# Expert 0's rows from a one-hot product in SBUF, and expert 0 run through before expert 1 starts

## What is computed

```python
h = rms_norm(x, norm_ffn_g)                      # 512 x 1024
g_idx = argmax(softmax(h @ w_rg + b_rg))         # one of 4 groups
top_p, top_i = top_k(softmax(expert logits of that group), 2)   # 2 of its 8 experts
for e in range(32):                              # rows given to expert e
    y = (silu(xb @ w1[e]) * (xb @ w3[e])) @ w2[e]    # w1, w3: 1024x512, w2: 512x1024
    out[rows of e] += weight * y
```

## Time and profile before

| | us |
|---|---|
| runs | 1755.36, 1760.81, 1761.26 |
| median | 1760.81 |
| the profiled execution, its own time | 1759.36 |
| its span, first to last instruction | 1757.8 |
| TensorE busy | 1610.4 (92%) |
| DMA, mean over the span | 185 GB/s |
| mean granted TensorE clock, share of full | 0.955 |

### The profile page before, as it was taken

The page is one execution under the profiler, slowest core; times in us unless marked ns, Lnnn a source line. Parts: engine busy times, 40 slices in busy tenths (PEclk is TensorE's granted clock), DMA queues, the critical chain, the costliest instruction groups (busy, mean ns, idle before and its releaser), DMA issues.

```text
span 1757.8 us, 15347 instructions
## 1 busy us (share of the span) xinstructions
PE 1610.4 (92%) x5808; PEld 792.1 (45%) x5808; DVE 723.0 (41%) x1529; ACT 478.5 (27%) x980; POOL 363.3 (21%) x348
## 2 busy tenths in 40 slices
PE   7998999999999699988888787899989999999998
PEld 3434456644554333333333333444455554445553
DVE  2856434264242312110110110549775143987612
ACT  2022242101121101100000001566366134735621
POOL 3800000001000111111211110148243012842500
PEclk9998999999999799998898888999999999999999
DMA  9511032457255599999999999602102130020101
GB/s 332 191 49 48 0 120 96 144 191 252 72 214 222 195 401 406 406 406 410 407 404 398 412 414 359 227 1 72 72 1 91 49 113 1 23 98 25 48 0 48
DMA packets 72401, 325.98 MB, mean 185 GB/s; under 512 B 10458, under 2 KB 13682, under 8 KB 59904
## 3 DMA queue, kind: packets, MB, share of 16 engines
q1 hardware_dynamic: 64976, 310.23, 45.3%
q0 software_dynamic: 6144, 10.52, 1.8%
q10 hardware_dynamic: 1200, 4.17, 0.6%
HBM read 320.60 MB, written 12.68 MB: 190 GB/s over the span
## 4 chain that ended last, share of the span: by engine, by line
PE 71%; DMA 21%; DVE 5%; ACT 2%; issue 1%; POOL 0%; SPq 0%; POOLq 0%; DVEq 0%; ACTq 0%
PE bank L190 67%; DMA arena<-in_w 16%; DMA arena<-x_rows,arena 3%; PE bank L2200 1%; DMA arena<-in_w_in 1%; DVE arena L2660 1%; DMA x_rows<-arena 1%; ACT arena L2375 1%; DVE arena L2647 0%; PE bank L680 0%; DVE arena L2662 0%; PE bank L929 0%; PE bank L2147 0%; DMA arena<-y_rows 0%; DMA y_rows<-arena 0%
## 5 line engine op out<-in xcount | busy, mean ns | idle before, releaser
L190 PE MATMUL bank<-arena 128*128 128x512 f32 (+10 forms) x4944 | 1507.8, 547 | 87.5 <-DMA arena<-in_w 51.1
L190 PEld LDWEIGHTS bank<-arena 128*128 128x128 f32 (+5 forms) x4944 | 689.0, 177 | 839.6 <-issue 780.3
L2822 POOL TENSOR_TENSOR arena<-arena 128x512 f32<-128x512 f32 x180 | 198.9, 1105 | 204.4 <-ACT arena L2428 186.7
L1834 DVE SCALAR_TENSOR_TENSOR arena<-arena,bank 64x512 f32<-64x512 f32 x32 | 24.0, 750 | 314.0 <-ACT arena L1247 314.0
L1891 POOL TENSOR_TENSOR arena<-arena 128x1 f32<-128x1 f32 (+2 forms) x44 | 34.2, 777 | 568.1 <-DVE arena L1282 341.3
L2428 ACT ACTIVATE arena<-arena 128x512 f32<-128x512 f32 x180 | 127.0, 725 | 21.1 <-POOL arena L2822 21.1
L1013 ACT COPY arena<-bank 128x512 f32<-128x512 f32 (+3 forms) x115 | 61.2, 539 | 234.1 <-PE bank L190 130.7
L1247 ACT ACTIVATE arena<-bank,arena 64x512 f32<-64x512 f32 x32 | 21.9, 684 | 362.2 <-PE bank L190 362.2
L1912 POOL DMA_INDIRECT y_rows<-arena x32 | 32.4, 1014 | 406.6 <-ACT arena L1258 245.7
L1294 DVE SCALAR_TENSOR_TENSOR arena<-arena 128x512 f32<-128x512 f32 x84 | 78.4, 933 | 2.7
L1827 DVE TENSOR_TENSOR arena<-bank,arena 128x512 f32<-128x512 f32 x32 | 22.1, 692 | 107.5 <-PE bank L929 107.5
(11 more groups left out here) (268 smaller groups left out, 898.1 us busy)
## 6 DMA issues: line engine op xcount, KB each, us to landing
arena<-in_w SPq DMA_DIRECT2D x96, 2048.0 KB, 39.8
arena<-in_w_in SPq DMA_DIRECT2D x15, 2048.0 KB, 9.4
arena<-in_w_ada SPq DMA_DIRECT2D x12, 2048.0 KB, 9.2
arena<-in_w_out SPq DMA_DIRECT2D x6, 2048.0 KB, 7.7
arena<-in_w_xk SPq DMA_DIRECT2D x2, 2048.0 KB, 9.3
arena<-in_w_xv SPq DMA_DIRECT2D x2, 2048.0 KB, 9.2
arena<-in_w_xq SPq DMA_DIRECT2D x2, 2048.0 KB, 9.9
arena<-in_w_xo SPq DMA_DIRECT2D x2, 2048.0 KB, 8.8
```

The costliest lines, as they stand in the source:

```text
L190: i = pe.e.matmul(o, l, r, start=first and j == 0, stop=last and j == len(pairs) - 1)
L2822: pool.e.tensor_tensor(yc, yc, k.prod[l][n % 4], ALU.add).then_inc(*k.pool.step("sum", l, f, j))
```

## The change

Expert 0 no longer has a gather. `dve_router_place` also builds, for each tile t, `OH0[t]` (128 tokens by 64 slots): the slot one-hot of the first choice times "this choice is expert 0", plus the same for the second choice. TensorE multiplies the rows of `x`, which are in SBUF, with it: 8 products per tile, accumulated over the four tiles in the bank `xT` of expert 0. These 32 products stand in three pieces in the router's tail: tiles 0 and 1 after the slots of group 1, tile 2 after the ranks of group 2, tile 3 after the slots of group 2. Then TensorE does up, gated and down of expert 0, then the rows of expert 1, and the skewed loop starts at expert 1. GpSimd gathers 1 and 2 first.

```diff
@@ memory
+    k.OH0 = [view(NFREE - 316 + 64 * t, 64) for t in range(3)]
+    k.OH0.append(k.ELT[:, 0:2, :].rearrange("p t e -> p (t e)"))
@@ new function
+def pe_first_rows(k, pe, u):
+
+    b = k.banks.at("xT", 0) if u else k.banks.take(pe, k.dve, "xT", 0, among=ROUTER_BANKS)
+    for t in GROUPS[u]:
+        pe.wait_ge(*k.dve.done("oh", t))
+        x = k.X[:, t, :].rearrange("p (q k) -> p k q", k=8)
+        for c in range(8):
+            i = product(pe, b[:, c * BLK:(c + 1) * BLK], [(x[:, c, :], k.OH0[t])], t == 0 and c == 0, t == 3 and c == 7)
+    if u == 2:
+        i.then_inc(*k.pe.step("xT", 0))
@@ pe_router
     pe_router_slots(k, pe, 1)
+    pe_first_rows(k, pe, 0)
     pe_router_ranks(k, pe, 2)
+    pe_first_rows(k, pe, 1)
     pe_router_slots(k, pe, 2)
+    pe_first_rows(k, pe, 2)
@@ pe_first
-    pe_expert_rows(k, pe, 0)
-    for e in range(NE + 1):
+    pe_expert_up(k, pe, 0)
+    pe_expert_gated(k, pe, 0)
+    pe_expert_down(k, pe, 0)
+    pe_expert_rows(k, pe, 1)
+    for e in range(1, NE + 1):
         if e + 1 < NE:
             pe_expert_rows(k, pe, e + 1)
-        if e:
+        if e > 1:
             pe_expert_gated(k, pe, e - 1)
         if e < NE:
             pe_expert_up(k, pe, e)
-        if e:
+        if e > 1:
             pe_expert_down(k, pe, e - 1)
@@ dve_router_place
+    dve.wait_ge(*V.last())
+    for t in GROUPS[u]:
+        dve.e.tensor_scalar(k.OH0[t], k.OHS[:, 2 * t, 0:BLK], k.AH[:, 2 * t, 0:1], None, ALU.mult).then_inc(*V.step())
+        dve.wait_ge(*V.last())
+        dve.e.scalar_tensor_tensor(out=k.OH0[t], in0=k.OHS[:, 2 * t + 1, 0:BLK], scalar=k.AH[:, 2 * t + 1, 0:1], in1=k.OH0[t],
+                                   op0=ALU.mult, op1=ALU.add).then_inc(*V.step("oh", t))
@@ dve_router_weights, part 0
+        dve.wait_ge(*P.done("cnt"))
@@ dve_first
     dve_expert_rows(k, dve, 0)
     for l in range(2):
         dve_mod_end(k, dve, l)
-    for e in range(NE + 1):
+    dve_router_weights(k, dve, 0)
+    dve_expert_up(k, dve, 0)
+    dve_expert_gated(k, dve, 0)
+    dve_expert_rows(k, dve, 1)
+    for e in range(1, NE + 1):
         if e + 1 < NE:
             dve_expert_rows(k, dve, e + 1)
-        if e:
+        if e > 1:
             dve_expert_gated(k, dve, e - 1)
@@ pool_gather
-    if e >= 2:
+    if e >= 3:
         pool.wait_ge(*k.pe.done("xT", e - 2))
@@ pool_first
-    pool_gather(k, pool, 0)
     pool_gather(k, pool, 1)
+    pool_gather(k, pool, 2)
     for e in range(NE + 1):
-        if e + 2 < NE:
+        if 3 <= e + 2 < NE:
             pool_gather(k, pool, e + 2)
```

More of the change, by code:

```diff
@@ L531, in sp_first @@
     R.ends[router] = [(P, ("xv", 3, 1))]
-    R.ends[residual] = [(k.x_out, ("x", 3)), (k.act, ("sq", "f", 3)), (P, ("tr", 3, 1))]
+    R.ends[residual] = [(k.x_out, ("x", 3)), (k.act, ("sq", "f", 3)), (P, ("xT", 0))]
     R.go_on([features, router, tokens, cross, ring[2], ring[3], ring[4], ring[0], ring[1], residual])
```

## The result

The changed kernel takes 1763.54 us in the median of 19 runs (1760.96 to 1766.03); the kernel before, on the same chip, 1758.05 (19 runs, 1755.36 to 1761.9). The ratio is **1.0029, 95% interval 1.0022 to 1.0037**: 5.1 us slower. The forecast was 6.1 us faster. The time lies in the range, but the sign is wrong. By the half per cent of the prediction it is no change; with 19 runs on either side it is a small, certain loss.

The account below looks back on a forecast made before the run. The DMA stream of expert weights was taken as the bound: full from 616.9 instead of 623.0, -6.1 us, so 1753.3 from the profiled 1759.4, or 1754.8 against the median; range 1750.5 to 1764.

Parts of the forecast that it names:

- the half per cent of the prediction: Whole kernel: about 0.5% (8.8 us) is what a measurement can tell from no change; chance of staying within it 0.74.
- a full stream of weights: Expert stage: its end is the end of the DMA weight stream, full from 616.9 instead of 623.0, 6.1 us earlier.
- TensorE's wait for the gather: Before up 0: expert 0's gather and 8 transposes go; up 0 starts at 592.5 instead of 601.8.
- VectorE's additions: Router's tail: two operations per tile, 0.2 to 0.25 us each, cost nothing; without cover at most 0.5 us per group.
- The 2.84 us from the end of up 0 to down 0: Expert 0's steps: 2.24 us from up 0 to the products after the gated transposes, plus 0.6 for a copy.
- rows of 1 and 2: Between down 0 and up 1: rows of experts 1 and 2 with the copy between, 2.05 us.
- up 1 with 7.0: Up products of expert 1: 7.0 us, from 608.5 to 615.5 instead of ending at 620.2.
- 32 products with 64 columns: Router's tail on TensorE: 64 records at 0.113 us, 7.2 us at full clock; 13.7 us at half.
- rival 1: Router's tail: half clock under the new products makes the kernel slower, +2.7 us, 1763.5; bad end 1768; chance 0.25.
- The order's price: Expert 0 through all steps first: 8.4 us from the end of up 0 to the start of up 1.
- up 0 itself: Up products of expert 0: 7.6 us instead of 9.15, ending at 600.1 instead of 610.93.
- 623.0: Weight stream: the time from which it was full before the change; predicted to move to 616.9, 6.1 us earlier.

Follow-up runs that it names:

- the contiguous, 128-wide form: Changed kernel with adjacent x columns as weights, old order behind up 0, and experts 0 and 1 both from the 32 products (gather 1 gone): ratio 0.9932, 1746.72 us.
- the contiguous, 64-wide form: Changed kernel with each x chunk 128 adjacent columns, not every eighth, and expert 0's w1 and w3 matched: ratio 0.9999; with old order 0.9955, again 0.9945.
- The overlooked line: Kernel before, with only the tenth weight load (w3 of expert 3) made to wait for expert 0's rows: ratio 0.998, again 0.9967.
- strided and 128 wide: Changed kernel with 128 columns per product instead of 64, the second half thrown away, weights still every eighth float: ratio 1.0016.
- the contiguous form with the order undone: Changed kernel with adjacent x columns as weights and the old skewed order put back behind up 0: ratio 0.9955, again 0.9945.

## Why the prediction was wrong

**Right.** That the expert stage is a full stream of weights whose end follows its start held in every run. TensorE's wait for the gather went. VectorE's additions hold nobody. The 2.84 us from the end of up 0 to down 0 (measured 2.86), rows of 1 and 2 with 2.05 us (1.91 and the start of up 1 behind it), up 1 with 7.0 (7.1) were all there. No gather that the change moved held TensorE, though the reason was not the one given: indices came 6.7 us later against T0 (the first gather at +15.3, before at +8.6), where the prediction had 0.1, and the gathers were fast.

**The step that failed** is "32 products with 64 columns", at 0.113 us a record. It was a mis-sized term: measured 0.238, so 15.2 us instead of 7.2, and with the ranks and slots between them the row from T0 to up 0 was 18.7 us and not 9.8. I wrote that no row has float32 products with these strided weights, and then took the value of contiguous ones. The strided row that I did look at was of transposes, 0.2 us each at half clock, and these cost no more than contiguous products do there (0.213): it could not show the price. The bound upward should have come from what was unknown, the stride, and not from what was known, the clock. The only place where it came up is half a clause of rival 1 ("by a third"). It was a factor of 2.1 at full clock.

**Rival 1** had nearly the right size for another reason. It asked for a mean of 0.16 us or more, and it put half clock as the cause. The clock was at half from 581.5 on, but at full clock the records were as far apart; the clock's own share is that up 0 took 9.52 us, where I had 7.6, and down 0 5.01 instead of 3.5. That the time of 1763.54 us lies inside the range, next to rival 1's 1763.5, is luck: rival 1 is 2.7 us above a kernel before of 1760.8, and measured are 5.1 us above one of 1758.05. The Trainium skill (TensorE: Matmul & The Clock Gate, section "Why this matters for your kernels") advises against idle gaps between matmul bursts. Here the gap was filled, TensorE was busy all the time from 578.4 to 596.2, and still the granted clock of that stretch was 0.59:

```profile
578.40:596.20 17.80, 17.80 (x80) 17.80 (x80) 6.12 (x30) 1.28 (x1) 3.53 (x4) 0.59 0.52 212
```

By that section alone it should have stayed up; the measurement decides. In the contiguous, 128-wide form it did stay at 1.00, and in one of the three profiles of the contiguous, 64-wide form. One row on the clock I had misread. The fall that I put under the 32 one-column records came behind them: they ran from 1359.65 to 1363.3, all at full clock, and the mean of 0.67 belongs to 1363 to 1365, which holds the last two or three of them, 0.65 us of idle time and four transposes.

```profile
1361.00:1363.00 2.00, 2.00 (x20) 2.00 (x19) 0.00 (x0) 0.00 (x0) 0.00 (x0) 1.00 0.00 0
```

So that row did not show what the prediction and its rival 1 took from it, that narrow work without gaps lets the clock fall. In the changed kernel the clock did fall without gaps; that the width was the reason is not shown.

**The order's price,** from the end of up 0 to the start of up 1, was 8.4 us in the prediction and 9.8 measured (16.9 less 7.1). The difference is down 0: 5.01 us instead of 3.5. It came after two idle stretches, 1.56 and 0.61 us, and the clock over it was 0.72. The mechanism was right; the part that was meant to pay for it did not come. Together: load 13 was to go out at 615.5, +32.8 from T0, and went at +45.1. Of these 12.3 us, 8.9 are the start of up 0, 1.9 up 0 itself, and the other 1.5 nearly all down 0.

**A smaller fault** is in the stream. I had counted from 623.0, when the stream of before was full, rather than from the issue at 620.24, and so 6.1 us for what by the issue is 4.8 us (620.24 - 615.5). Measured, the end follows the issue: 450.8 and 450.7 us. From the full stream to the landing it would be 448.0 before and 449.3 after. Why the issue is the better mark was not looked into.

**The overlooked line** changed neither sign nor size for the worse, by the run of it in the kernel before; the changed kernel can't be run without it. It does make my account of the gathers in the changed kernel wrong, in their favour: 1 and 2 landed 2.9 us after their issue, and not 8.4.

**Left open.** Why strided weights cost 0.238 us for products and nothing extra for transposes: the runs show the price, not its cause, and no stride other than eight floats was tried. Why the clock fell in two of the three profiles of the contiguous, 64-wide form and not in the third is open as well. The late tenth load together with the best form needs no run of its own, as that form has it; what the form would bring without it is not known.

## What to carry to other kernels

Price a new instruction by rows that match it in how its operands are laid out, not only in shape; where no row does, put the unmatched property itself between two bounds, because it can be a factor of two. When a change buys an earlier start by giving up an overlap, work out each half by itself: here the overlap given up was sure to cost 7.5 us, and the gain hung on one guess. And before a gather on the critical path is replaced, look at what runs beside it: holding back one 2 MB load by 5 us made the kernel faster (0.998 and 0.9967), where the 32 products of this change, as they were first written, gained nothing.

## What the runs showed that I had not expected

- A strided weight load of a float32 product: 0.238 us from record to record at full and at half clock, with 64 and with 128 columns. Contiguous: 0.112 at full clock at either width, and 0.213 at half with 64 columns (128 were not seen at half clock).
- A gather of 64 rows of 4 KB took 3.0 us with the DMA engines otherwise nearly idle, and 7.8 to 8.4 us beside one weight load (9.1 in the median in the second profile of the contiguous form with the order undone).
- The granted clock can fall under a TensorE that is never idle: 0.50 from 582 to 596 in the changed kernel. It differs between profiles of the same products: contiguous and 64 wide it was 0.50 from 590 to 593 in one and 1.00 through the whole tail in another; contiguous and 128 wide, 1.00 in all of the router's tail in the one profile taken; strided and 128 wide, 0.50 from 584 to 587 and 1.00 behind it.
